# Three reorderings in a hybrid decoder step: an earlier weight cast, a positional term carried as matmul columns, and two exponents moved ahead of a query copy

## What is computed

```python
h = modulate(rms_norm(x, norm_attn), sh1, sc1)
parts = split_in(h @ w_in)                     # q, three key/value pairs, gates, HGRN2 inputs, ...
q, k = rope(rms_norm(...)), rope(rms_norm(...))
# compress_one: blocks of 32 rows every 16 rows, through a two-layer network
w    = w1.reshape(2, 16, d, 64)
proj = einsum('bnsgd,rsdh->rbngh', sub, w)     # sub: rows in groups of 16
hid  = einsum('rsd,rsdh->h', pe, w)            # positional term, one vector for every block
hid  = hid + proj[0, :, 0:nc] + proj[1, :, 1:1+nc]
kc   = gelu(hid) @ w2
# attention: compressed, selected and window branches, each a masked softmax
```

## Time and profile before

| | |
|---|---|
| median of three runs | 2223.75 us |
| the profiled execution | 2223.62 us |
| its span, first to last instruction | 2221.7 us |
| mean granted TensorE clock | 0.978 |
| busy: PE, DVE, ACT, POOL | 96%, 53%, 30%, 26% |
| projections, compression, attention begin | 55, 252, 363 us |

### The profile page before, as it was taken

One profiled execution on the slowest core, in us unless ns is written; L12 is line 12 of the kernel. 1 busy time (PEld: TensorE's weight loads), 2 busy tenths in 40 slices (PEclk: granted clock), 3 DMA queues, 4 the chain that ended last, 5 costly groups with the idle time before them and its releaser, 6 DMA issues.

```text
span 2221.7 us, 34227 instructions
## 1 busy us (share of the span) xinstructions
PE 2139.2 (96%) x13417; PEld 1959.7 (88%) x13417; DVE 1183.1 (53%) x2162; ACT 672.5 (30%) x1411; POOL 587.8 (26%) x367
## 2 busy tenths in 40 slices
PE   8999998999989999999999999999999999999999
PEld 3788886676666899999999999999999999999998
DVE  5774275888976167664211333655445444454445
ACT  3332365777763034332002112321110011100112
POOL 0112212545651156541000113421221112211120
PEclk9999998999999999999999999999999999999999
DMA  9021353000036312222232543221111111111112
GB/s 362 19 98 39 95 176 137 1 1 1 1 102 214 120 29 59 59 59 78 68 92 79 176 109 99 79 66 39 58 38 39 57 38 58 39 42 54 39 39 79
DMA packets 175588, 168.60 MB, mean 76 GB/s; under 512 B 10194, under 2 KB 156083, under 8 KB 170116
## 3 DMA queue, kind: packets, MB, share of 16 engines
q1 hardware_dynamic: 167462, 117.96, 17.8%
q0 software_dynamic: 7760, 48.55, 6.6%
q10 hardware_dynamic: 224, 0.08, 0.0%
HBM read 152.98 MB, written 17.87 MB: 77 GB/s over the span
## 4 chain that ended last, share of the span: by engine, by line
PE 62%; DVE 2%; issue 0%; POOL 0%; ACT 0%; POOLq 0%; ACTq 0%
PE psall L244 19%; PE psall L246 18%; PE psall L245 18%; PE psall L2460 3%; PE psall L2092 2%; DVE work L2338 1%; PE psall L2119 1%; DVE work_short L2658 0%; DVE work L2646 0%; POOL work L2014 0%; PE psall L2134 0%; PE psall L2101 0%; PE psall L3196 0%; PE psall L2127 0%; PE psall L2136 0%
## 5 line engine op out<-in xcount | busy, mean ns | idle before, releaser
L244 PE MATMUL psall<-hT_short,ring_short 128*128 128x344 f32 x1896 | 614.2, 324 | 1.6 <-DVE work_short L2658 0.6
L246 PE MATMUL psall<-hT_short,ring_short 128*128 128x344 f32 x1896 | 607.0, 320 | 0.0
L239 POOL TENSOR_TENSOR ring_short<-ring,ring_short 128x1024 fp32r<-128x1024 f32 (+3 forms) x52 | 196.8, 3785 | 1069.0 <-DVE ring_short L234 760.4
L245 PE MATMUL psall<-work_short,ring_short 128*128 128x344 f32 x1392 | 445.3, 320 | 0.0
L244 PEld LDWEIGHTS psall<-hT_short,ring_short 128*128 128x128 f32 x1896 | 358.3, 189 | 2.5 <-issue 1.5
L246 PEld LDWEIGHTS psall<-hT_short,ring_short 128*128 128x128 f32 x1896 | 357.6, 189 | 0.0
L245 PEld LDWEIGHTS psall<-work_short,ring_short 128*128 128x128 f32 x1392 | 262.2, 188 | 0.2
L3357 DVE SCALAR_TENSOR_TENSOR xT<-psall,mod,xT 128x344 f32<-128x344 f32 (+1 forms) x264 | 151.2, 573 | 132.6 <-PE psall L246 129.2
L245 PE MATMUL psall<-xT_short,ring_short 128*128 128x344 f32 x648 | 207.8, 321 | 0.0
L3237 ACT ACTIVATE work<-psall 128x344 f32<-128x344 f32 (+1 forms) x66 | 30.1, 458 | 504.5 <-PE psall L246 503.6
L244 PE MATMUL psall<-work_short,work_short 128*128 128x344 f32 x528 | 177.1, 335 | 2.8 <-POOL work_short L239 2.2
(11 more groups left out here) (476 smaller groups left out, 4003.7 us busy)
## 6 DMA issues: line engine op xcount, KB each, us to landing
ring<-in_w_up SPq DMA_DIRECT2D x44, 512.0 KB, 5.0
ring<-in_w_in SPq DMA_DIRECT2D x27, 512.0 KB, 3.9
work<-in_ada_w SPq DMA_DIRECT2D x23, 512.0 KB, 4.4
work<-in_w_down SPq DMA_DIRECT2D x10, 1024.0 KB, 5.0
ring<-in_ada_w SPq DMA_DIRECT2D x9, 512.0 KB, 4.2
x_spill<-xT SPq DMA_DIRECT2D x4, 1032.0 KB, 15.0
xT<-x_spill SPq DMA_DIRECT2D x4, 1032.0 KB, 7.2
ring<-in_ada_w SPq DMA_DIRECT2D x4, 1024.0 KB, 14.6
```

Source lines behind the costliest of these rows:

```text
L239: return eng.tensor_tensor(lo, src, hi, ALU.subtract)
L244: pe.matmul(out, w[0], x[0], start=first, stop=False)
L245: pe.matmul(out, w[0], x[1], start=False, stop=False)
L246: return pe.matmul(out, w[1], x[0], start=False, stop=last)
```

## The change

In the projections DVE takes the high part of the next group's weights ahead of the group's unit 4 (its fifth), not its unit 6. In the compression `terms()` goes away: DVE writes the two halves of the positional rows as two more columns behind the 64 columns of each group of each prompt operand, and the first mix for keys and for values carries them along (66 columns each). The two results are added for a = 0 and a = 1 apart, in `lift_gelu` and `add` of the prompt. In the attention ACT does the exponents of items 0 and 1 ahead of `queries(1)` and of the high part of the compressed values.

```diff
             for u in range(3 * NT):
-                if u % NT == 6:
+                if u % NT == 4:
                     wait(v, mm, (u // NT) * NT)
                     weights.take_high(v, u // NT + 1)
...
-    def pipeline(eng, first, second, third, terms, keys=None, before=None, between=None):
+    def pipeline(eng, first, second, third, keys=None, before=None, between=None):
         first(0, 0, NSUB_P)
         first(0, 1, NSUB_P)
-        terms()
         second(0, 0, NSUB_P)
...
-        def terms():
-            pe.wait_ge(pe_read, 1)
-            pe.wait_ge(inputs.weights_in, 64)
-            for a in range(2):
-                for e in range(8):
-                    last = pe.matmul(pe_ps[:, a, :], w1[:, a, e, :], peT[:, a, :, e], start=(e == 0), stop=(e == 7))
-            last.then_inc(pe_terms, 1)
-            pe.wait_ge(w2_in, 48)
...
+            if prompt(q):
+                pe.wait_ge(pe_read, 1)
+                pe.wait_ge(inputs.weights_in, 64)
+                n += 2
             out = view(s.ps[4 + a], 0, NG, P)[:, :, 0:n]
             for e in range(8):
                 last = pe.matmul(out, w1[:, a, e, :], pairs[a][:, :, e, 0:n], start=(e == 0), stop=(e == 7))
...
+            if prompt(q):
+                pe.wait_ge(w2_in, 48)
             pe.wait_ge(gelu, 2 * q + a + 1)
...
-            act.wait_ge(pe_terms, 2)
-            act.activation(pe_late[0:HD, :], pe_ps[HD:P, :, 1], ACT.Copy).then_inc(pe_moved, 1)
-            act.wait_ge(pe_read, 2)
...
+            if prompt(q):
+                act.activation(pe_late[0:HD, a:a + 1], src[HD:P, 0, NSUB_P + 1:NSUB_P + 2], ACT.Copy).then_inc(pe_moved, 1)
+                act.wait_ge(pe_read, a + 2)
             act.activation(lifted[a][0:HD, :, 0:m], src[HD:P, :, 1:n], ACT.Identity,
                            bias=pe_h[0:HD, a:a + 1]).then_inc(lift, 1)
...
-        v.tensor_copy(view(s.ring, R, 32), s.ps[6][:, 0:32]).then_inc(pe_read, 1)
-        def terms():
-            v.wait_ge(pe_moved, 1)
-            v.tensor_tensor(pe_h[0:HD, :], pe_ps[0:HD, :, 0], pe_late[0:HD, :], ALU.add).then_inc(pe_read, 1)
+        for a in range(2):
+            for g in range(NG):
+                last = v.tensor_copy(pairs[a][:, g, :, NSUB_P:NSUB_P + 2],
+                                     s.ps[6][:, 16 * a:16 * a + 16].rearrange("p (r e) -> p e r", r=2))
+        last.then_inc(pe_read, 1)
...
+            if prompt(q):
+                v.wait_ge(pe_moved, a + 1)
+                v.tensor_tensor(pe_h[0:HD, a:a + 1], src[0:HD, 0, NSUB_P:NSUB_P + 1], pe_late[0:HD, a:a + 1],
+                                ALU.add).then_inc(pe_read, 1)
             v.wait_ge(lift, 2 * q + a + 1)
...
             compress.scalar(act, lambda: queries(0))
+            for i in range(EARLY):
+                exponent(i)
             queries(1)
             act.wait_ge(compress.placed, compress.PLACED)
...
                 if what == "exponent":
-                    exponent(i)
+                    if i >= EARLY:
+                        exponent(i)
```

More of the change, by code:

```diff
@@ L865, in compress_programs @@
     pairs = [view(s.ring, 2048 * a, NG, 8, P) for a in range(2)]
-    peT = view(s.ring, R, 2, 2, 8)
     pe_h, pe_late = view(s.ring, R + 32, 2), view(s.ring, R + 34, 2)
@@ L877, in compress_programs @@
     pe_terms, pe_read, pe_moved = s.sem("c_pe_terms"), s.sem("c_pe_read"), s.sem("c_pe_moved")
-    pe_ps = s.ps[7][:, 0:4].rearrange("p (a r) -> p a r", r=2)
-    def pipeline(eng, first, second, third, terms, keys=None, before=None, between=None):
+    def pipeline(eng, first, second, third, keys=None, before=None, between=None):
         first(0, 0, NSUB_P)
         first(0, 1, NSUB_P)
-        terms()
         second(0, 0, NSUB_P)
@@ L910, in nothing, with prompt @@
         pass
+    def prompt(q):
+        return isinstance(q, int) and q == 0
     def sync(sp):
@@ L974, in make @@
             last.then_inc(made, 1)
-        pipeline(pe, turn, mix, make, terms, between=between)
+        pipeline(pe, turn, mix, make, between=between)
     def evacuate(eng, copy, done, banks):
@@ L1010, in scalar @@
         pipeline(act, evacuate(act, lambda o, i: act.activation(o, i, ACT.Copy), evac_a, (1, 3)), lift_gelu, nothing,
-                 terms, keys=lambda: splits.place_keys(act, 0, 1), before=before)
+                 keys=lambda: splits.place_keys(act, 0, 1), before=before)
     def vector(v, before, between):
@@ L1015, in vector @@
         v.wait_ge(pe_terms, 1)
-        v.tensor_copy(view(s.ring, R, 32), s.ps[6][:, 0:32]).then_inc(pe_read, 1)
-        def terms():
-            v.wait_ge(pe_moved, 1)
-            v.tensor_tensor(pe_h[0:HD, :], pe_ps[0:HD, :, 0], pe_late[0:HD, :], ALU.add).then_inc(pe_read, 1)
+        for a in range(2):
[3 more added lines that the diff above has]
+        last.then_inc(pe_read, 1)
         def add(q, a, n):
             m = n - 1
+            src = view(s.ps[4 + a], 0, NG, P)
+            if prompt(q):
+                v.wait_ge(pe_moved, a + 1)
+                v.tensor_tensor(pe_h[0:HD, a:a + 1], src[0:HD, 0, NSUB_P:NSUB_P + 1], pe_late[0:HD, a:a + 1],
+                                ALU.add).then_inc(pe_read, 1)
             v.wait_ge(lift, 2 * q + a + 1)
             wait(v, gelu, 2 * q + a - 1)
-            src = view(s.ps[4 + a], 0, NG, P)
             v.tensor_tensor(hid[a][0:HD, :, 0:m], src[0:HD, :, 0:m], lifted[a][0:HD, :, 0:m],
@@ L1041, in place @@
             last.then_inc(placed, 1)
-        pipeline(v, evacuate(v, v.tensor_copy, evac_v, (0, 2)), add, place, terms,
+        pipeline(v, evacuate(v, v.tensor_copy, evac_v, (0, 2)), add, place,
                  keys=lambda: splits.lower_keys(v, 0, 1), before=before, between=between)
```

## The result

The changed kernel takes 2204.15 us (median of three runs, 2203.48 to 2208.9) against 2223.75. The medians lie 19.6 us apart; the ratio is 0.9919, 95% interval 0.9902 to 0.9935, which is 18 us, or 0.8%, faster. The forecast was 2207.4. The profiled execution is the slowest of the three, 2208.9 us with a span of 2207.0, so the comparison of traces explains 14.7 us of span, and the rest has to come from other executions.

The account below looks back on a forecast made before the run. PE, busy for 96% of the span, was taken as the bound: its own work plus holes and the low clock behind some. Terms 7.7 + 5.0 + 3.5 = 16.2 us off 2223.6 gave 2207.4, range 2204 to 2212.

Parts of the forecast that it names:

- the likeliest case: Whole kernel: the forecast of 2207.4 us holds, own range 2204 to 2212; chance 0.60.
- the three terms: Projections, compression and attention: 7.7 + 5.0 + 3.5 = 16.2 us off the profiled execution's 2223.6.
- Edit 1: Projections, cast two units earlier: PE's waits at group starts go, 7.7 us, ends 6.0 and 9.2.
- The wait for unit 13: Projections, group 1 to 2: PE waits 2.4 us behind unit 16 because DVE delivers unit 13 late.
- The group 0 part: Projections, group 0 to 1: the 0.81 us hole goes, DVE's lock hidden; otherwise at most 0.8 us lost.
- Edit 2: Compression, positional term: 6.98 us of PE work go, but PE waits 1.2 us for rows; gain 5.0 us.
- both lower ends: Compression, positional term: gain 2.7 us if rows take 7.9 us, 3.3 if the clock drops for the second mix.
- Edit 3: Attention, two exponents first: exponent 0 and the maximum of item 2 come sooner, 3.5 us, ends 2.2 and 3.7.
- The later clock: Low clock after 420 us costs 25 us and falls differently when everything starts earlier: 3 us either way, outside the sum.
- waits did take the place of waits: Rival: unit 13's wait drops the clock, rows land late, second mix is slow; 2214 to 2218, chance 0.22.
- The compression's loop never stayed at the low clock: Rival, compression loop, 270 to 360 us: clock stays low, steps take up to twice as long; chance 0.04.
- Nothing further on absorbed the gain: Rival, behind the attention's start: window copies or a weight load don't move, PE waits; 2220 to 2228, chance 0.07.

Follow-up runs that it names:

- all again: The full changed kernel run once more, with nothing further changed, against the kernel before: 2204.64 us, ratio 0.9924.
- before again: The kernel before, unchanged, as a run of its own against itself: 2221.95 us, ratio 0.9995.
- The first trace: Profiled execution of the changed kernel's first measurement, all three edits against the kernel before: 2208.9 us, span 2207.0.
- The three edits alone: Three kernels, each with one edit against the kernel before: cast 2211.48 us, positional term 2216.57, exponents 2216.50.
- The trace of edit 3: Trace of the kernel before with only the two exponents moved first: 2216.50 us, ratio 0.9967; its span is 9.6 us shorter.
- That of edit 2: Trace of the changed kernel with cast and exponents taken back, only the positional term changed: 2216.57 us, ratio 0.9970; span 2.7 us shorter.

## Why the prediction was right

The time, 2204.15, lies in the likeliest case's own range, 2204 to 2212, but at its edge, 3.3 us under the forecast; that it is inside owes something to luck. The same kernel's later medians are 2206.14 and 2204.64. The mechanism held: the sum of the three terms (16.2 us) is near to what "all again" shows against "before again": 9.1 + 4.9 + 3.8 = 17.8 us of span.

- **Edit 1, 7.7 us forecast, about 9 measured in the stage.** The wait for unit 13 came where it was forecast. It is 1.64 + 0.39 us, not 2.4 + 0.3, for the most part because PE came to it at 146.76 and not at 146.2. The term mis-sized is the clock: I took 1.65 us for a drop behind that wait, and in the changed kernel none followed (1.00 from 152 us on). That is the upper end I gave, 9.2. The group 0 part was wrong in small, and why PE came late to unit 13: the 0.81 us went, but 1.01 us of waiting for ACT's evacuation came at unit 7, more than the 0.8 I allowed for. ACT's queue has the square of the decode unit (L734, 118.35) ahead of that evacuation (L691, 119.17), and the square waits for DVE's sum (L777, 117.64). With the low part on DVE, which frees DVE sooner, the wait is gone.
- **Edit 2, 5.0 us forecast.** Five traces with full clock in the transposes and the second mix give 15.0 to 15.1 us from first transpose to third mix against 20.1, so 5.0. Two with slow transposes (16.7 and 16.8) give 3.3 to 3.4, what I had for a slow mix. The first trace (19.1) gives 1.0, below both lower ends, 2.7 and 3.3: its rows were late and the clock low for transposes and mix together. Taking the upper end was right in most traces, but not for my reason. I let the length of the hole decide the clock, and the clock is low before the hole; holes of 0.94 and 1.01 us had slow transposes behind them, one of 1.61 had not. The wait for the rows was 0.94 to 2.2 us (1.2 forecast) where the loads were not moved.
- **Edit 3, 3.5 us forecast, 3.8 measured.** The table load does stand ahead of the wait. The maximum of item 2 stands behind the low part of the values, as forecast; not said was that PE's wait for POOL behind it would grow by 1.8 us, to 2.75. The drain of 1380 ns that the Trainium skill, ScalarE: Activation LUTs, section What ACT_TABLE_LOAD costs, adds to a switch does not show here either: exponent 0 starts 1.30 us after the load does. The prediction's estimate with it was 1.8.
- **The later clock**, 3 us either way, was too narrow for a single execution: unchanged stages differ by up to 7 us between traces. It was wide enough for the medians.
- Of the rivals, waits did take the place of waits in the first trace, without reaching the time given for it. The compression's loop never stayed at the low clock. Nothing further on absorbed the gain.

The three edits alone give 12, 7 and 7 us, 26 in sum, and together 17 to 18. By their own stages they give 18 as well (9 + 5 + 4), so the surplus of the lone edits lies in stages that they do not touch. The trace of edit 3 shows that, with 5.5 us. That of edit 2 does not: its later stages are longer. These are medians of 5 to 11 executions, so luck in single executions does not explain the surplus; where it comes from is open.

## What to carry to other kernels

Where an early step of a shared engine is moved to remove a wait, ask what it holds while it runs, and for how long: here POOL's subtraction holds DVE's operations with both inputs in SBUF until it ends, and the wait came back two microseconds long at the unit that DVE then delivered late. Price a removed piece of PE work by what comes next to be waited for, not by its own length: 7 us of matmuls were worth 5, because the rows that PE needs next come 5.6 to 6.9 us behind an issue that did not move. And before believing in an effect of under some 7 us that one pair of traces shows, compare the stages that the edit does not touch.

## What the runs showed of the hardware

- The granted clock is a part of the result that does not repeat. The same program had its second mix at 1.2 GHz in one execution (3.05 us) and at 2.4 in two others (1.97); with the transposes ahead of it that is 2.8 us in one place.
- In the projections the clock fell behind holes of 2.2 and 2.65 us (casts at units 5 and 2) and of 3.84 and 2.76 us (the kernel before), and did not behind holes of 0.81, 1.01 and 1.64 us. In the compression the length of the hole for the rows does not tell the clock behind it: it was full behind 1.61, 1.21 and 0.97 us and low behind 0.94, 1.01 and 2.22, and it was low ahead of all of them.
- DVE operations with both inputs in SBUF were held for as long as a POOL subtraction of 3264 columns ran (6.16 us for a pair that takes 0.5). One with an input in PSUM was not: L819 took 0.42 us while POOL ran. With the subtraction on DVE itself the same work took half POOL's time (3.56 against 7.2 us).
